# Inverse levels, decay scores and the scaling of W_out in another order in the mixing phase of a hybrid GLA and Gated DeltaNet block

## The reference

```python
# p: projections; states of context are the start of the latent scans; d = 0 forward, 1 backward
def gla_chunked(q, k, v, log_a, S0):       # 4 heads, DK 64, DV 128
    b = cumsum(log_a in the chunk)
    scores = sum_d q_i k_j exp(b_i - b_j), causal
    o = scores @ v + (q exp(b)) @ S_prev;  S = exp(b_last) S_prev + (k exp(b_last - b))^T v
def gdn_chunked(q, k, v, log_alpha, beta, S0):   # 4 heads, 128 x 128, chunk 64
    L = strict_lower(beta_i * (k_i . k_j) * exp(g_i - g_j));  A = I + L
    U = A^-1 (beta v);  W = A^-1 (beta exp(g) k)
    delta = U - W S;  o = (q exp(g)) S + Aqk delta;  S = a S + (k exp(g_last - g))^T delta
def merge_heads(o_gla, o_gdn, p, gla_norm_g, gdn_norm_g, w_out):
    ya = rmsnorm(o_gla, gla_norm_g) * silu(gate_gla);  yb = rmsnorm(o_gdn, gdn_norm_g) * silu(gate_gdn)
    return concat([ya, yb]) @ w_out
x = x + gt1 * merge_heads(...);  x = x + gt2 * mlp(norm(x))
```

## Time and profile before

| | us |
|---|---|
| median of 3 runs (lowest, highest) | 1847.55 (1845.86, 1849.35) |
| the profiled execution | 1851.97 |
| its span, first to last instruction | 1850.0 |
| TensorE busy | 1599.8 (86%) |
| VectorE, ScalarE, GpSimd busy | 1003.2, 640.3, 434.4 |
| mean granted TensorE clock | 0.94 of 2.4 GHz |

### The profile page before, as it was taken

One profiled execution on the slowest core, in us unless ns is written; L12 is line 12 of the kernel. 1 busy time (PEld: TensorE's weight loads), 2 busy tenths in 40 slices (PEclk: granted clock), 3 DMA queues, 4 the chain that ended last, 5 costly groups with the idle time before them and its releaser, 6 DMA issues. The chain is left out here.

```text
span 1850.0 us, 35180 instructions
## 1 busy us (share of the span) xinstructions
PE 1599.8 (86%) x15022; PEld 1347.8 (73%) x15022; DVE 1003.2 (54%) x1536; ACT 640.3 (35%) x976; POOL 434.4 (23%) x381
## 2 busy tenths in 40 slices
PE   5699999999947878777777399779999998899997
PEld 2467887999947777777777288658888877787876
DVE  2444542011115665666665754855545478987875
ACT  3366344221102222222222222545545453332433
POOL 1301111111104355554443511313222200000000
PEclk9699999999978998999998599989999999999999
DMA  7213333436543333333311432123544577352522
GB/s 298 73 51 94 117 92 97 147 100 194 172 113 98 86 94 93 93 93 94 93 59 36 159 131 73 65 85 126 169 144 150 163 255 273 114 205 93 192 91 91
DMA packets 169565, 229.81 MB, mean 124 GB/s; under 512 B 34189, under 2 KB 101121, under 8 KB 168386
## 3 DMA queue, kind: packets, MB, share of 16 engines
q1 hardware_dynamic: 162562, 205.79, 34.4%
q0 software_dynamic: 6848, 21.76, 3.7%
HBM read 165.78 MB, written 61.73 MB: 123 GB/s over the span
## 5 line engine op out<-in xcount | busy, mean ns | idle before, releaser
L87 PE MATMUL fps<-xh_m,w1r_hi 128*128 128x512 f32 x448 | 177.8, 397 | 19.5 <-DVE w1r_lo L2477 5.9
L87 PE MATMUL fps<-bh,ah 128*128 128x512 f32 x448 | 176.4, 394 | 14.3 <-DVE acc L2630 9.9
L88 PE MATMUL fps<-xl_m,w1r_hi 128*128 128x512 f32 x448 | 176.2, 393 | 0.0
L89 PE MATMUL fps<-xh_m,w1r_lo 128*128 128x512 f32 x448 | 176.1, 393 | 0.0
L88 PE MATMUL fps<-bl,ah 128*128 128x512 f32 x448 | 175.7, 392 | 0.0
L89 PE MATMUL fps<-bh,al 128*128 128x512 f32 x448 | 175.7, 392 | 0.0
L80 PE MATMUL ps_main<-hhi,whi 128*128 128x512 f32 (+3 forms) x360 | 137.2, 381 | 15.6 <-DVE wlo L647 11.8
L81 PE MATMUL ps_main<-hlo,whi 128*128 128x512 f32 (+3 forms) x360 | 133.8, 372 | 0.0
L82 PE MATMUL ps_main<-hhi,wlo 128*128 128x512 f32 (+3 forms) x360 | 133.7, 371 | 0.0
L80 PE MATMUL ps_main<-whi,hhi 128*128 128x256 f32 x416 | 120.0, 288 | 0.0
L2277 ACT ACTIVATE ah<-araw 128x2048 fp32r<-128x2048 f32 x28 | 53.7, 1917 | 186.4 <-PE fps L89 122.8
(11 more groups left out here) (305 smaller groups left out, 3622.5 us busy)
## 6 DMA issues: line engine op xcount, KB each, us to landing
s_hid<-hb SPq DMA_DIRECT2D x112, 256.0 KB, 2.3
araw<-s_hid SPq DMA_DIRECT2D x28, 1024.0 KB, 6.7
w1raw<-in_w_ff SPq DMA_DIRECT2D x16, 1024.0 KB, 6.3
w2b<-in_w_ff SPq DMA_DIRECT2D x16, 1024.0 KB, 6.8
raw<-in_w_in SPq DMA_DIRECT2D x14, 1024.0 KB, 5.3
wa<-in_w_ada SPq DMA_DIRECT2D x8, 1024.0 KB, 10.3
z_sb<-in_w_ada SPq DMA_DIRECT2D x16, 512.0 KB, 4.3
n_sb<-in_w_ada SPq DMA_DIRECT2D x16, 512.0 KB, 4.4
```

The lines of the kernel that those rows point to most:

```text
L87: pe.matmul(out, lhi, rhi, start=start, stop=False, skip_group_check=True)
L88: pe.matmul(out, lhi, rlo, start=False, stop=False, skip_group_check=True)
L89: return pe.matmul(out, llo, rhi, start=False, stop=stop, skip_group_check=True)
```

## The change

- W_out gets a buffer of all eight parts (K.wraw) that is there from the mixing on. SP issues one part at the end of each of the steps 0 to 7, and VectorE scales it two iterations later (scale_weight), between level_add(p, 1) and state(r, 1). The rows of gt1 and gt2 are made at the start of mixing, in the banks po and pr. To make room, kint shares its tile with trix and chunk, and the tiles ones, cols, csil and sel end with the projection; one column of cols is copied for the MLP.
- VectorE's list in a step: level_add(1) before state(r, 1); differ_level one at a time between level_mask and level_add of the levels 2 to 4; accumulates spread. ScalarE takes decay_level 3 to 5 before keys_out. TensorE takes the first scores after level_p(3), turn_keys and scores(p, 0, 1) after level_y(5), scores(p, 1, 1) after level_p(5).
- states(p) goes over both chunks in turn, product by product.
- In the merge, no loading, scaling or rows; the low parts of W_out go to GpSimd for k = 1, 3, 5 and to VectorE for the others, and states(2) and scale(1) stand after low(0) on VectorE.

```diff
+            dve.tensor_copy(K.mod[:, 32:40, 1], K.cols[:, 56:64])
             dve.tensor_tensor(K.mod[:, 16:48, 0], ps_sq[:, 1, :NLATE], K.cols[:, 16:48], ALU.add)
...
-        tri, trix = m.sb("tri", [P, 2, P]), m.sb("trix", [P, 2, P])
-        chunk = m.sb("chunk", [P, 2, P])
+        tri, kint = m.sb("tri", [P, 2, P]), m.sb("kint", [P, 2, 2, P])
+        trix, chunk = kint[:, 0], kint[:, 1]
...
+            def out_weight(k):
+                if k >= 2:
+                    sp.wait_ge(wo_scaled, k - 1)
+                sp.dma_start(K.wraw[:, k], A["w_out"][k * P:(k + 1) * P]).then_inc(ld_wo[k % 2], 16)
...
+                        for i, n in enumerate(("gla_norm_g", "gdn_norm_g")):
+                            sp.dma_start(ngain[:, i:i + 1], A[n].rearrange("a n -> n a")).then_inc(ld_ngain, 16)
+                    if p < KT:
+                        out_weight(p)
             steps(step)
...
+                act.wait_ge(rows_done, x + 1)
+                dst = gt1 if x < 2 else K.gt2
+                act.activation(dst[:, (x % 2) * 512:(x % 2 + 1) * 512], (po + pr)[x][:], ACT.Copy).then_inc(row_out, 1)
 
...
                         decay_queries(p)
-                    keys_out(p)
-                    if lat(p):
                         for lev in range(3, LEVELS):
                             decay_level(p, lev)
+                    keys_out(p)
                     for c in R2:
                         states_out(p, c)
...
+            def scale_weight(k):
+                dve.wait_ge(ld_wo[k % 2], 16 * (k // 2 + 1))
+                if k == 0:
+                    dve.wait_ge(ld_ngain, 32)
+                    dve.wait_ge(row_out, 2)
+                w = K.wraw[:, k]
+                dve.scalar_tensor_tensor(w, w, ngain[:, k // NH:k // NH + 1], gt1[:], ALU.mult, ALU.mult).then_inc(wo_scaled, 1)
...
                 if r is not None:
+                    if 2 <= r + 1 < KT + 2:
+                        scale_weight(r - 1)
                     state(r, 1)
                 if p is not None:
-                    level_add(p, 1)
                     if lat(p):
-                        for lev in range(3):
-                            differ_level(p, lev)
+                        differ_level(p, 0)
                     level_mask(p, 2)
+                    if lat(p):
+                        differ_level(p, 1)
+                        differ_level(p, 2)
+                    level_add(p, 2)
                 if r is not None and lat(r):
                     outputs(r)
                 if p is not None:
-                    level_add(p, 2)
                     level_mask(p, 3)
+                    level_add(p, 3)
                     if lat(p):
                         accumulate(p, 0, 0)
+                        differ_level(p, 3)
+                    level_mask(p, 4)
+                    if lat(p):
+                        differ_level(p, 4)
+                        differ_level(p, 5)
+                    level_add(p, 4)
+                    if lat(p):
                         accumulate(p, 1, 0)
-                    level_add(p, 3)
-                    if lat(p):
-                        for lev in range(3, LEVELS):
-                            differ_level(p, lev)
-                    level_mask(p, 4)
-                    level_add(p, 4)
                     level_mask(p, 5)
                     if lat(p):
                         accumulate(p, 0, 1)
+                    level_add(p, 5)
+                    if lat(p):
                         accumulate(p, 1, 1)
-                    level_add(p, 5)
...
             last.then_inc(g_ready, 1)
+            def rows(x):
+                for i in range(4):
+                    c = (16 if x < 2 else 40) + 4 * (x % 2) + i
+                    last = pe.matmul((po + pr)[x][:, i * P:(i + 1) * P], K.mod[:, c, 0:1].broadcast_to([P, P]), K.ident[:],
+                                     start=True, stop=True)
+                last.then_inc(rows_done, 1)
+
+            rows(0)
+            rows(1)
             pe.wait_ge(sm_act, 4)
             for x, cols in enumerate((gcol, K.beta, egc)):
                 last = pe.transpose(pg[1][:80, x * P:(x + 1) * P], cols[:].rearrange("p d t h -> p (d t h)"), K.ident[:])
             last.then_inc(rt_ready, 1)
+            rows(2)
+            rows(3)
             pe.wait_ge(init_done, 1)
...
                     after(pe, st_done[d], 2 * s + n)
+                if s == 0 and n == 0:
+                    pe.wait_ge(row_out, 4)
                 for h in range(NH):
...
 
-            def states(s, c):
+            def states(s):
                 pe.wait_ge(kt_out, s + 1)
                 pe.wait_ge(ld_gv, 16 * (s + 1))
                 if lat(s):
-                    pe.wait_ge(acc_done[1 - c], 2 * (s - TC + 1))
+                    pe.wait_ge(acc_done[0], 2 * (s - TC + 1))
+                    pe.wait_ge(acc_done[1], 2 * (s - TC + 1))
                 for z in R2:
                     for hd in range(NH):
                         a, x = hd // 2, hd % 2
-                        last = pe.matmul(pg[1 - c][half(x), head(2 * z + a)], kint[half(c), z, a, half(x)], gva[half(c), hd],
-                                         start=True, stop=True)
-                last.then_inc(gs_ready[c], 1)
+                        for c in R2:
+                            last = pe.matmul(pg[1 - c][half(x), head(2 * z + a)], kint[half(c), z, a, half(x)], gva[half(c), hd],
+                                             start=True, stop=True)
+                            if z == 1 and hd == NH - 1:
+                                last.then_inc(gs_ready[c], 1)
...
                     level_p(p, 2)
                     level_y(p, 3)
+                    level_p(p, 3)
                     if lat(p):
                         scores(p, 0, 0)
                         scores(p, 1, 0)
-                    level_p(p, 3)
                     level_y(p, 4)
+                    level_p(p, 4)
+                    level_y(p, 5)
                     turn_keys(p)
-                    level_p(p, 4)
                     if lat(p):
                         scores(p, 0, 1)
-                    level_y(p, 5)
+                    level_p(p, 5)
                     if lat(p):
                         scores(p, 1, 1)
-                    level_p(p, 5)
-                    for c in R2:
-                        states(p, c)
+                    states(p)
                     if lat(p):
...
             def low_w(k):
                 pool.wait_ge(wo_hi, k + 1)
-                pool.tensor_tensor(wlo[:, k], wraw[:, k % NW], whi[:, k].bitcast(F32), ALU.subtract).then_inc(wo_lo, 1)
+                pool.tensor_tensor(wlo[:, k], wraw[:, k], whi[:, k].bitcast(F32), ALU.subtract).then_inc(wo_lo_pool, 1)
 
             def gate(t):
                 pool.wait_ge(ld_gates[t % 2], 16 * (t // 2 + 1))
                 pool.wait_ge(sq_done, t + 1)
                 pool.tensor_tensor(K.xo[:, tile(t)], K.xo[:, tile(t)], gates[:, t % 2], ALU.mult).then_inc(gated, 1)
 
-            low_w(0)
             low_w(1)
-            low_w(2)
             gate(0)
             low_w(3)
-            low_w(4)
             low_w(5)
             gate(1)
-            low_w(6)
-            low_w(7)
             for t in range(2, TL):
                 gate(t)
...
             def high_w(k):
-                act.wait_ge(wo_scaled, k + 1)
-                act.activation(whi[:, k], wraw[:, k % NW], ACT.Copy).then_inc(wo_hi, 1)
+                act.activation(whi[:, k], wraw[:, k], ACT.Copy).then_inc(wo_hi, 1)
...
-            sq_x1 = wraw
-            for r in range(4):
-                act.wait_ge(rows_done, r + 1)
-                dst = gt1 if r < 2 else K.gt2
-                act.activation(dst[:, (r % 2) * 512:(r % 2 + 1) * 512], row_bank[r], ACT.Copy).then_inc(row_out, 1)
-            high_w(0)
+            for k in range(3):
+                high_w(k)
             square(0)
-            high_w(1)
-            high_w(2)
+            high_w(3)
             rsqrt(0)
-            high_w(3)
-            square(1)
             high_w(4)
             high_w(5)
-            rsqrt(1)
+            square(1)
             high_w(6)
             high_w(7)
+            rsqrt(1)
             high(0)
-            act.wait_ge(wo_lo, KT)
...
+            def low_w(k):
+                dve.wait_ge(wo_hi, k + 1)
+                dve.tensor_tensor(wlo[:, k], wraw[:, k], whi[:, k].bitcast(F32), ALU.subtract).then_inc(wo_lo_dve, 1)
...
-            dve.wait_ge(row_out, 2)
-            scale_w(0)
+            low_w(0)
             add_states(0)
             states(1)
-            scale_w(1)
+            low_w(2)
             variance(0)
-            scale_w(2)
             add_states(1)
-            scale_w(3)
             scale(0)
-            scale_w(4)
+            low_w(4)
             variance(1)
+            low_w(6)
+            low(0)
+            low_w(7)
             states(2)
-            scale_w(5)
-            scale_w(6)
```

(41 more changed lines are left out.)

39 lines of the change are left out of this document (13 added, 26 removed).

## The result

| | before | after |
|---|---|---|
| median, us (runs, lowest to highest) | 1848.45 (4, 1845.86 to 1849.58) | 1797.51 (4, 1795.54 to 1799.86) |
| ratio, 95% interval | | 0.9732 (0.9715 to 0.9749) |
| profiled execution, its span | 1851.97, 1850.0 | 1795.54, 1793.5 |
| mean granted TensorE clock in that execution | 0.94 | 0.951 |

The change takes 51 us, 2.7%; 1798.0 was predicted, within 1780 to 1822.

A forecast was written before the change was run, and what follows sets the result against it. Mixing was taken as bound by a ring of hand-overs between engines, the merge by a nearly empty head, then TensorE. Terms -17.3 - 33.2 - 1.0 + 1.5 + 0.2 = -49.8 from 1847.55 gave 1798 us, range 1780 to 1822.

The forecast's parts named there:

- The head: Start of the merge: first product with W_out 30.0 us after the phase's start instead of 47.0; 17.3 in the sum.
- The body: Rest of the merge, bound by TensorE (106 of 109 us busy): no gain of its own, its end moves with its first product.
- The latent steps: Eight mixing steps: the new order and less clock loss gain 4.15 us each after linear's wait, 33.2 in all.
- the cold stretch: Latent steps: TensorE's clock falls after waits; one such stretch of two goes, with 1.8 us a step for further ones.
- Rival 1: Latent steps: cold stretches stay or contention eats half the gain; steps gain 1 to 3 us, 1815 us; 25%.
- The scaling: Latent steps: scale_weight costs 1.27 us on VectorE, between level_add(1) and the state sum, ahead of level_mask(2).
- States alternating: End of a latent step: both state copies begin together, linear starts 0.2 us later; four tiles in parallel could save up to 0.4.
- The small terms: Second context step gains 1.0 us; start of mixing loses 1.5 to rows(0), rows(1); the copy ending the projection costs 0.2.
- The loads of W_out: Mixing: eight more loads of 512 KB on SP cost zero; up to 1.8 us a step if scale_queries waits for egb.
- rival 3: Mixing: W_out's load delays egb and decay rows, scale_queries waits, each step loses 3 us; slower, 1855 us; 4%.
- Rival 2: Mixing: VectorE's own sequence is the ring, TensorE's wait only changes its name, steps gain nothing; 1831 us; 8%.
- Rival 4: Latent steps: the clock stays up and the four tiles overlap, steps gain 6.2 us; 1781 us; 8%.

The follow-up runs named there:

- e11: The changed kernel run again, unaltered: 1800.11 us, ratio to the kernel before 0.9722 to 0.9758.
- e2: The changed kernel with the old order of mixing, states chunk by chunk too, so only W_out's part of the change remains: 1826.74 us.
- e1: The kernel before with only the new order of mixing and states alternating; W_out still loaded, scaled and split in the merge: 1821.53 us.
- e3: The changed kernel with the products of states chunk by chunk again instead of alternating: 1800.98 us.
- e6: The changed kernel with states(2) moved ahead of scale(0) in VectorE's list of the merge: 1797.55 us.
- e12: The kernel before with a pad of 32 bytes ahead of wohi and wolo and one behind them: 1847.99 us.
- e7: The changed kernel with scale_weight ahead of advance(p), unread TensorE products in five gaps per latent step, and states(2) ahead of scale(0) in the merge: 1783.16 us.
- e9: The changed kernel with scale_weight ahead of advance(p) and states(2) ahead of scale(0) in the merge, without unread products: 1797.68 us.

## Why the prediction was right, and where its steps were not

The parts below are those of the two profiled executions. They come to 54.3 us, where the sum had 49.8. The spans differ by 56.5: mixing also began 2.8 us earlier (ScalarE's aB at 541.08, before 543.91), which is not the change's doing, since e11 has it at 543.71 and e2 at 540.39, and the MLP was 0.5 longer. By the medians it is 51 us. So the mechanism is the one predicted, but that the forecast met the median to 0.5 us is luck: the terms are off by 0.9 to 2.6 us each, not all the same way.

**The head** was given 17.3, though the layout itself makes 17.0 (47.0 less 30.0), and gave 19.3. The queue of the two engines was the right picture, down to inter(2) behind states(2); it was laid out too slow. scale(0) was over at 14.6 us (layout 16.0), GpSimd's gate(1) at 20.1 (22.05), low(0) at 22.5 (24.6), and the rest followed at its distance. The clock was down for inter(0) and inter(2), as taken.

**The body** was given nothing, and gave 2.6: 2.2 from the products' spacing, some 0.8 because five instead of nine products ran at the low clock at its start, less 0.4 that the stretch behind the last product became longer. This is the term that was missing.

**The latent steps** were given 4.15 each and gave 3.9 in the profiled runs (27.1 over seven periods, and 4.1 in the first latent step). The layout put a step with a full clock at 41.9, and 42.75 with outputs(r); 42.48 and 43.36 were measured. Its first half fits to 0.1: level_y(2) 0.96 and level_p(2) 3.31 after the start of answer(r, 1) were laid out, 0.92 and 3.23 came. The missing 0.6 gathered from level_p(4) on: in the step of the first 42.48, states began 23.56 after the start of answer(r, 1), where the layout had 23.01. Two errors nearly cancel: the order is worth a little less than thought, the clock a little more. Its loss fell by 13.7 over seven periods, 2.0 each, where 1.8 was the term. But that this term came out was a piece of luck: one execution of e1, with nearly the same order, lost 23.1, one of e3 18.3, the change 11.9 and 13.7, and e6 with the change's mixing 6.8. The prediction treated the cold stretch as a thing that a step has or hasn't; the runs show it as a matter of chance, whose odds differ with the list. Rival 1 was in that sense partly true in every run.

**The scaling** was laid out at its full 1.27 on the ring in the new order; 0.75 was measured there, and nothing in the old.

**States alternating.** 0.2 a step was taken off for linear's wait; the start of linear moved by 0.02 (1.89 against 1.87 in e3). By the Trainium skill, TensorEngine Tiling (Array Packing), section Tiling Modes, the four tiles can work at once; the row agrees in part, 1.59 to 1.10 and not to 0.8, and the wait for the copy takes all of it.

**The small terms.** The second context step gave 1.9 instead of 1.0. The start of mixing was given a loss of 1.5 and lost 0.6 from ScalarE's aB to the first difference of GpSimd: the transposes did wait behind rows(0) and rows(1) and began 1.0 later behind aB, and a part of that was made up by the transposes themselves, which took 0.27 each instead of 0.42 to 0.44. The ScalarE copies of the rows are hidden.

**The loads of W_out** were given nothing, and cost nothing that shows, but rival 3's first link is there. In four latent steps of the change scale_queries on GpSimd waits for egb, 5.2 us in all; the kernel before, e1 and e12, without loads of W_out in the mixing, have no such wait.

```profile
750.33 2.35 POOL L1099 TENSOR_TENSOR qc<-qc,egb 128x1024 f32<-128x1024 f32 x1 [1.77 <-DMA egb<-s_row]
```

It doesn't reach TensorE: this step's period is one of the two of 42.48, and no load is among TensorE's waits.

**The other rivals.** Rival 2 has little in the profile: TensorE's idle time shrank by 11.8 us over the seven periods and did not only change its name. Rival 4's 1781 is what a mixing with the clock up and a shorter head gives, as e7 shows with 1783, though not by the four tiles.

## What to carry to other kernels

Price a stall on TensorE's ring twice: once as time, once as a chance that the clock falls for some us behind it. The second differs from run to run and hid a saving of an estimated 9 us in e9; one profile of each kernel can't tell it from the effect of an edit, so take several runs. Where a ring of hand-overs can't be closed, shorten it and fill the gaps with unread products together: either alone gave nothing here, both gave 14 us. Weights made ready at the head of a phase that TensorE bounds are worth moving ahead of it: all 19 us by which the first product came earlier reached the end.

## What was not expected of the hardware

- Identical products with identical shapes ran every 233, 227 or 229 ns, with the clock at 1.00, depending on where tiles lie.
- Two profiled executions of one kernel agreed to 0.03 us in periods without a fall of the clock, and had their falls in different steps; a period with one was 1.4 to 4.4 us longer. The same gap of 1.41 us stood ahead of a fall in the one and of none in the other.
- A group of four small VectorE updates (1.25 us) waited through three GpSimd operations in a row and took 6.83.
